# Scaling the far probabilities of every attention head: GpSimd multiplications or ScalarE copies with a row scale

## The reference, cut to what matters

```python
DILATED = ((128, 1), (512, 4), (2048, 16))

def combine_by_denominator(branches):
    outs = jnp.stack([o for o, _ in branches], axis=0)
    lses = jnp.stack([l for _, l in branches], axis=0)
    wts = jax.nn.softmax(lses, axis=0)
    return jnp.sum(wts[..., None] * outs, axis=0)

    # in hybrid_layer, for the prompt
    branches = [dilated_branch_prompt(qa, ka, va, w, r) for (w, r) in DILATED]
    o_a = combine_by_denominator(branches).reshape(bsz, s, A_WIDTH) * jax.nn.silu(ga.astype(jnp.float32))
```

## Time and profile before

| | |
|---|---|
| time, median of 3 runs | 1589.83 us (1588.72 to 1597.04) |
| profiled execution, its own time | 1592.49 us |
| its span, first to last instruction | 1590.8 us |
| mean granted TensorE clock | 0.979 |
| PE busy | 1520.6 us (96%) |
| DVE busy | 973.1 us (61%) |
| ACT busy | 844.6 us (53%) |
| POOL busy | 555.1 us (35%) |

### The profile page before, as it was taken

How to read it: one execution, slowest core, us unless ns; L and a number is a source line. 1 busy time by engine, 2 the same in 40 slices (tenths; PEclk the granted TensorE clock), 3 DMA queues, 4 the chain that set the end, 5 groups by cost and what they waited for, 6 DMA issues and landing times. The chain is left out here.

```text
span 1590.8 us, 40209 instructions
## 1 busy us (share of the span) xinstructions
PE 1520.6 (96%) x16265; PEld 1329.7 (84%) x16265; DVE 973.1 (61%) x2100; ACT 844.6 (53%) x1625; POOL 555.1 (35%) x664
## 2 busy tenths in 40 slices
PE   7999999999999999999999997899999889999997
PEld 6998889999998999989898987896777567787775
DVE  4437766433377878788787773337666667455642
ACT  5437777222376666678888882446777511111110
POOL 1102221200165655556565652305565421121110
PEclk9999999999999999999999999897999999999999
DMA  6310011135413122121211111649990475866651
GB/s 241 105 54 30 32 46 63 62 94 144 122 46 79 43 57 76 46 77 32 69 40 54 47 40 58 159 114 212 270 227 21 137 250 171 274 198 214 224 181 40
DMA packets 197526, 177.06 MB, mean 111 GB/s; under 512 B 85059, under 2 KB 181918, under 8 KB 195038
## 3 DMA queue, kind: packets, MB, share of 16 engines
q1 hardware_dynamic: 197342, 174.49, 38.1%
HBM read 124.75 MB, written 52.94 MB: 112 GB/s over the span
## 5 line engine op out<-in xcount | busy, mean ns | idle before, releaser
L49 PE MATMUL f_bank<-c_ht,c_whi 128*128 128x384 f32 (+1 forms) x864 | 310.3, 359 | 0.2
L51 PE MATMUL f_bank<-c_ht,c_wlo 128*128 128x384 f32 (+1 forms) x864 | 301.4, 349 | 0.5 <-issue 0.5
L50 PE MATMUL f_bank<-c_ht,c_whi 128*128 128x384 f32 (+1 forms) x864 | 301.1, 349 | 0.4 <-issue 0.4
L633 POOL TENSOR_TENSOR f_scr<-f_scr 128x192 f32<-128x192 f32 (+1 forms) x180 | 112.9, 627 | 210.1 <-PE f_tps L1294 207.8
L49 PEld LDWEIGHTS f_bank<-c_ht,c_whi 128*128 128x128 f32 x864 | 162.1, 188 | 15.0 <-DVE c_wlo L929 2.5
L50 PEld LDWEIGHTS f_bank<-c_ht,c_whi 128*128 128x128 f32 x864 | 162.3, 188 | 10.8 <-issue 1.9
L51 PEld LDWEIGHTS f_bank<-c_ht,c_wlo 128*128 128x128 f32 x864 | 162.2, 188 | 8.7
L49 PE MATMUL a_s<-a_whi,a_mhi 128*128 128x512 f32 (+1 forms) x306 | 124.6, 407 | 6.5 <-DVE a_y L2527 6.5
L50 PE MATMUL a_s<-a_wlo,a_mhi 128*128 128x512 f32 (+1 forms) x306 | 121.4, 397 | 0.0
L878 ACT ACTIVATE f_scr<-f_scr 128x384 f32<-128x384 f32 (+1 forms) x180 | 92.4, 537 | 38.7 <-POOL f_scr L634 38.2
L1088 DVE COPY_PREDICATED f_scr<-f_scr,f_tps 128x384 f32<-128x384 int32 (+1 forms) x150 | 94.6, 630 | 22.7 <-PE f_tps L1294 7.4
(11 more groups left out here) (401 smaller groups left out, 3812.8 us busy)
## 6 DMA issues: line engine op xcount, KB each, us to landing
f_wraw<-in_w_in SPq DMA_DIRECT2D x27, 512.0 KB, 4.1
zs<-f_stage SPq DMA_DIRECT2D x48, 192.0 KB, 2.5
a_k<-in_ck SPq DMA_DIRECT2D x48, 192.0 KB, 5.2
a_v<-in_cv SPq DMA_DIRECT2D x48, 192.0 KB
f_scr<-in_xp SPq DMA_DIRECT2D x16, 512.0 KB, 4.1
a_x<-in_xp SPq DMA_DIRECT2D x16, 512.0 KB, 5.9
out_y_prompt<-a_y SPq DMA_DIRECT2D x16, 512.0 KB, 3.2
zt<-f_stage SPq DMA_DIRECT2D x38, 192.0 KB, 1.8
```

The costliest lines, as they stand in the source:

```text
L49: nc.tensor.matmul(out, w_hi, m_hi, start=start, stop=False)
L50: nc.tensor.matmul(out, w_hi, m_lo, start=False, stop=False)
L51: return nc.tensor.matmul(out, w_lo, m_hi, start=False, stop=stop)
L633: G.tensor_tensor(d[:, :, hs:], b[:, :, hs:], r, ALU.subtract)
```

## The change

The four far multiplications of each head leave GpSimd. ScalarE does them as 16 copies in place, one for each class `m` and row block `i`, with a per-row scale read from `wt`. They are a new entry `zf` of the list, four per head, each of four copies of one `i`: after units k = 5 (width 128), 6 (256), 7 (512) and 9 (384) of the next head, ahead of the turn of the same place; for the last head after the fourth, fifth and sixth of the remaining turns. A new semaphore `far_scaled` counts them. GpSimd keeps the six near multiplications, without the far ones between them.

```diff
         if h and k in (merged, spread):
             order.append(("x" if k == merged else "z", h - 1))
+        if h and k in (5, 6, 7, 9):
+            order.append(("zf", 4 * (h - 1) + (5, 6, 7, 9).index(k)))
...
         if n in (1, 3):
             order.append(("x" if n == 1 else "z", NH - 1))
+        order.extend(("zf", 4 * (NH - 1) + x) for x in {3: (0,), 4: (1,), 5: (2, 3)}.get(n, ()))
...
-        def scaled_by(h, i, far, m):
-
-            part = min(m, 2) if (far, i) == (0, 0) else 0
-            return len(SCALES) * h + SCALES.index((far, i, part)) + 1
+        NEARS, FARS = [s for s in SCALES if not s[0]], [s for s in SCALES if s[0]]
+
+        def scaled_blocks(eng, h, blocks):
+
+            scales = [(far, i, min(m, 2) if (far, i) == (0, 0) else 0) for i, far, m, _ in blocks]
+            near, far = [s for s in scales if not s[0]], [s for s in scales if s[0]]
+            if near:
+                eng.wait_ge(S["scaled"], BASE + len(NEARS) * h + max(NEARS.index(s) for s in near) + 1)
+            if far:
+                eng.wait_ge(S["far_scaled"], BASE + len(FARS) * h + max(FARS.index(s) for s in far) + 1)
...
-                    for far, i, part in SCALES:
-                        if far:
-                            pool.wait_ge(S["weights"], BASE + h + 1)
-                            p, m0 = pfs[h % 2][i][:], 0
-                        elif i == 0:
+                    for far, i, part in NEARS:
+                        if i == 0:
...
+                elif kind == "zf":
+                    h, i = n // len(FARS), FARS[n % len(FARS)][1]
+                    act.wait_ge(S["weights"], BASE + h + 1)
+                    for m in range(NC):
+                        p = pfs[h % 2][i][:, m, :]
+                        ins = A(p, p, ACT.Copy, scale=wt[h % 2][:, 1, m * SB + i:m * SB + i + 1])
+                    ins.then_inc(S["far_scaled"], 1)
...
                 if h >= 2:
-                    dve.wait_ge(S["scaled"], BASE + len(SCALES) * (h - 1))
+                    dve.wait_ge(S["scaled"], BASE + len(NEARS) * (h - 1))
+                    dve.wait_ge(S["far_scaled"], BASE + len(FARS) * (h - 1))
...
-                    pe.wait_ge(S["scaled"], BASE + max(scaled_by(h, i, far, m) for i, far, m, _ in blocks))
+                    scaled_blocks(pe, h, blocks)
```

More of the change, by code:

```diff
@@ L1683, in attend_project @@
         S = {n: sem("a_" + n) for n in ("iota", "mask", "q_first", "q_near", "scores", "shifted", "exped", "own",
-                                        "masks", "far_out", "far_in", "back_out", "back_in", "apart", "expw", "weights", "scaled", "turned", "copied_a", "copied_v", "used", "final",
+                                        "masks", "far_out", "far_in", "back_out", "back_in", "apart", "expw", "weights", "scaled", "far_scaled", "turned", "copied_a", "copied_v", "used", "final",
                                         "held")}
```

## The result

The kernel takes 1624.86 us, the median of four executions (1619.51 to 1628.52), beside 1593.43 us for the kernel before on the same chip: a ratio of 1.0193, with a 95% interval of 1.0142 to 1.0243. That is some 31 us slower. The forecast was 1615, and the time lies 0.9 us above its range of 1602 to 1624. The forecast added its change to 1589.83 us, the median then on record for the kernel before; 3.6 us of the distance between forecast and time are this base, and some 6 us are the change (31.4 where 25.5 was forecast).

What follows compares the result with a forecast made beforehand. PE was taken to bound the kernel while heads run, the other engines after the last head. Stalls 23.8 plus clock 2.8 less 1.1 at the end gave +25.5 us on 1589.8: 1615 us, range 1602 to 1624.

Steps and rivals of the forecast that it cites:

- Heads 0 to 4 gain nothing from GpSimd's relief: While heads run, PE sets the pace and GpSimd's scaling is covered, so removing its far multiplications gives nothing.
- The price of a copy: On ScalarE, 0.31, 0.41, 0.52 and 0.63 us for widths 128 to 512: 7.5 us a head, bounds 5.1 and 8.9.
- The stalls and their places: PE waits for ScalarE's late group copies: 2.6, 5.5, 5.1, 5.5, 5.1 us in heads 1 to 5, together 23.8.
- The second stalls: PE waits again before groups 19 (1.8 us) and 38 (0.6 us), partly swallowed by the slow clock.
- The clock: PE at half clock some 3 us behind long stalls: 0.3 us each in heads 2, 4, 1.1 in 3, 5; 2.8 together.
- The upper bound of the prediction: For the slow clock in the heads: 1.7 us for each of five stalls, 8.5 us.
- After the last head: Freed low parts of w_out against a 3.3 us PE wait at group 92: 1.1 us gained; bounds 3 gained, 1 lost.
- The sum: Whole kernel: stalls 23.8 plus clock 2.8 less 1.1 at the end, +25.5 us, giving 1615 us.
- D: Rival: copies without overlap, or a slow clock after every stall: +30 to +37 us, about 1623; chance 0.13.
- A: Rival: the same stalls in the heads, but the clock stays high: +22.7 us, 1612.5; chance 0.27.
- B: Rival: cheap copies at the unscaled spacing, stalls 12.9 us less 2 at the end: +11, 1601; chance 0.12.
- C: Rival: ScalarE's lateness never reaches PE at groups 16 and 34, the end gains 3 us: 1587; chance 0.03.

Runs made afterwards that it cites:

- fill kernel: The changed kernel with 8 to 32 spare identity transposes ahead of PE's waits of groups 2, 18, 19, 36, 54, 55 and 72: 1614.95 us, ratio 1.0149.
- the second run: The changed kernel run again, unaltered, on the chip of the fill kernel: 1623.56 us, ratio 1.0208 against the kernel before.
- experiment 6: The changed kernel with each block of four copies behind the turn of its place instead of ahead of it: 1618.0 us, ratio 1.0165.

## Why the prediction was wrong in size and right in kind

- **Heads 0 to 4 gain nothing from GpSimd's relief.** Right: without any far scaling the heads keep their distances to 0.1 us from head 2 on.
- **The price of a copy.** Right: 7.5 us a head forecast, and 1.17 + 1.60 + 2.45 + 2.03 = 7.25 us measured from start to start in head 3 of after.
- **The stalls and their places.** Right: groups 2, 18 and 19, 36 and 92, with 2.05, 3.48 and 1.23, 3.96, and 3.16 us, where 2.6, 3.7 and 1.8, 4.5, and 3.3 stood, so each was taken 0.1 to 0.6 us too long. The second stalls are partly swallowed by the slow clock, as forecast: before group 38 no wait is left in after, and the fill kernel shows 0.39 us, where 0.6 was forecast. The sum of the stalls, 23.8, is best compared with the fill kernel, where nothing of the clock is mixed in: 23.2.
- **The clock: the step that failed.** "I read it as lasting some 3 us", and from it 0.3 us in heads 2 and 4 and 1.1 in heads 3 and 5, 2.8 in all. It cost 7.3 us in this execution (30.5 - 23.2) and 8.6 in the medians. That it would come was right; its length was mis-sized. After group 18's stall it lasted 6.8 us and not 3, so it slowed the work behind the second stall too, which the sum had taken to run at full speed. Head 1 had no clock term at all, and behind its stall of 2.05 us the clock fell for 3.4 us (not so in the second run). By head, after less fill, from starts to 0.01 us: 1.5, 2.2, 2.0, 0.7, 0.9. The upper bound of the prediction, 1.7 for each of five stalls or 8.5, was the better reading. The 3 us were taken from one slow stretch of before, at the end, which did last 3.4 us with PE busy throughout. One stretch doesn't tell how long the next will be: those of after lasted 3.4 or 6.8 us.
- **After the last head.** A gain of 1.1 us was forecast and 0.3 lost. Its own chain held: step 10's product stands 23.9 us behind the last weights, where it was 24.65, so 0.75 us came. But from that product to the projection it took 14.3 us instead of 13.3. In the trace the reload of the mixed tile is issued 4.7 us after its store (1301.18 and 1296.46), where it was 3.4 before (1274.06 and 1270.63). The prediction had let this stretch follow unchanged. It isn't shown that the change lengthened it: experiment 6's kernel has the same work at the end and took 12.9 us for it, the second run of the changed kernel 14.7, and the others between 12.0 and 14.4.
- **The sum.** 23.2 + 7.3 + 0.3 = 30.8 us, beside some 31 measured. The forecast was 25.5: 4.5 of the difference is the clock's term, 1.4 the end's, less 0.6 for the stalls. That the time left the range is partly the base's doing: 31.4 us on the base of the forecast, 1589.83, would be 1621.3.
- **The rivals.** D, slow clock at every stall, was nearest, for its second half alone. A (clock stays high) is what the fill kernel builds, and there its +22.7 us is met by +23.5 (1614.95 less 1591.42). B fell with the price of 7.25. C fell with 23.6 us of waits where 2.0 stood.

Two things stay open: what decides whether a slow stretch lasts 3.4 or 6.8 us, and how much of experiment 6's 5.6 us is clock.

## What to carry to other kernels

Cost added work on an in-order engine by the backlog that it puts ahead of the next result somebody waits for, and not by the engine's average share: ScalarE had 7 us idle in each head, and 7.5 us of new work in four blocks still cost 30.5 us over five heads, 7.3 of it by the clock, while the same copies one by one cost 8.5. Look for the due times on both sides of the new work, of what stands behind it and of the work itself. A stall on a busy TensorE should be costed at its length and again with the slow clock that may come with it: here each stall of 3.2 to 4.0 us inside the heads had one, shorter ones some of the time, and it cost 1.5 us a head on the average and up to 2.2. And ask first whether the relieved engine was ever waited for: here in one head of six, and there eight copies were enough.

## What the runs showed of the hardware

- Transposes that nobody reads, put where PE would have stood still, made the kernel 8.6 us faster (1614.95 instead of 1623.56) with the granted clock at 1.00 from 1093 to 1273 us.
- A stall's length alone doesn't say whether the clock falls. In the kernel without row scale, 2.43 us of idleness in head 2 left it at 1.00, and the same 2.43 us in head 4 (from 1198.8 to 1201.3) was followed by 0.50. The windows of that kernel:

```profile
1128.00:1134.00 6.00, 4.25 (x36) 3.25 (x38) 1.96 (x8) 5.48 (x19) 2.02 (x2) 1.00 1.01 225
...
1204.00:1206.00 2.00, 1.73 (x10) 1.43 (x10) 0.74 (x3) 2.00 (x8) 0.00 (x0) 0.50 0.03 8
```

- A per-row scale from memory costs ScalarE 91 to 95 ns an instruction on every width measured: 389 and 298, 498 and 403, 605 and 512, 710 and 616 ns for 128, 256, 384 and 512 columns, with it and without.
